# Start addresses of the weight blocks in the on-chip ring

## The reference

```
x = x + mixed(h @ w_in) @ w_out
x = x + memory_cross_attention(h, mem_n, w_xq, w_xkv, w_xo)
x = x + (silu(gate) * up) @ w_down        # gate, up = split(conv(h @ w_up) + bias)
x = x + (fox_attention(...)  * silu(gate)) @ fox_w_out
x = x + (swa_attention(...)  * silu(gate)) @ swa_w_out
```

## Time and profile before

| | |
|---|---|
| timed runs, us | 2169.78, 2170.08, 2170.18 (median 2170.08) |
| span of the profiled execution, us | 2167.6 |
| TensorE matmuls, busy | 2156.3 us, 13406 instructions |
| VectorE, ScalarE busy | 1618.3 us, 1327.2 us |
| read from HBM | 384.34 MB |

### The profile page before, as it was taken

How to read it: one execution, slowest core, us unless ns; L and a number is a source line. 1 busy time by engine, 2 the same in 40 slices (tenths; PEclk the granted TensorE clock), 3 DMA queues, 4 the chain that set the end, 5 groups by cost and what they waited for, 6 DMA issues and landing times.

```text
span 2167.6 us, 34503 instructions
## 1 busy us (share of the span) xinstructions
PE 2156.3 (99%) x13406; PEld 1865.8 (86%) x13406; DVE 1618.3 (75%) x2945; ACT 1327.2 (61%) x2601; POOL 9.7 (0%) x22
## 2 busy tenths in 40 slices
PE   9999999999999999999999999999999999999998
PEld 8888888888888888888888888888888888888887
DVE  7898666786688877655778867777676767688774
ACT  7866447775576666544666656555556655567764
POOL 0000000000000000000000000000000000000000
PEclk9999999999999999999999999999999999999999
DMA  7443434665455555555555555545554455544453
GB/s 279 169 146 137 147 115 141 218 217 186 156 190 189 188 191 186 193 185 192 187 191 189 185 194 185 193 171 197 181 177 174 167 192 186 189 161 155 146 200 140
DMA packets 107619, 389.31 MB, mean 180 GB/s; under 512 B 12304, under 2 KB 12560, under 8 KB 106688
## 3 DMA queue, kind: packets, MB, share of 16 engines
q1 hardware_dynamic: 105264, 377.31, 50.2%
q0 software_dynamic: 1904, 9.47, 1.2%
q10 hardware_dynamic: 288, 0.32, 0.0%
HBM read 384.34 MB, written 2.13 MB: 178 GB/s over the span
## 4 chain that ended last, share of the span: by engine, by line
PE 95%; DVE 3%; ACT 1%; issue 0%; DMA 0%; SPq 0%; DVEq 0%; ACTq 0%
PE main L510 88%; PE two L510 6%; PE two L513 1%; DVE WL L987 1%; DVE gt L987 0%; DMA RAW<-ws 0%; DVE GQ L993 0%; ACT L1654 0%; ACT WH L1655 0%; DVE GK L993 0%; PE main L556 0%; ACT PP L1655 0%; DVE PB L987 0%; ACT NT L1655 0%; DVE PP L993 0%
## 5 line engine op out<-in xcount | busy, mean ns | idle before, releaser
L1655 ACT ACTIVATE WH<-RAW 128x512 fp32r<-128x512 f32 x1416 | 882.1, 629 | 657.6 <-PE main L510 651.1
L987 DVE TENSOR_TENSOR WL<-RAW,WH 128x512 fp32r<-128x512 f32 x1416 | 961.2, 687 | 383.9 <-ACT WH L1655 374.4
L510 PE MATMUL main<-A,WH 128*128 128x512 f32 (+1 forms) x3680 | 1141.9, 393 | 1.0 <-DVE WL L987 1.0
L510 PEld LDWEIGHTS main<-A,WL 128*128 128x128 f32 x3584 | 673.9, 188 | 154.8
L510 PE MATMUL main<-A,WL 128*128 128x256 f32 x3584 | 713.7, 278 | 0.0
L510 PEld LDWEIGHTS main<-A,WH 128*128 128x128 f32 x3680 | 562.7, 189 | 13.8 <-issue 9.3
L510 PE MATMUL main<-H,WH 128*128 128x512 f32 x704 | 221.1, 395 | 0.0
L510 PE MATMUL main<-B,WH 128*128 128x512 f32 (+1 forms) x640 | 184.4, 373 | 0.0
L510 PEld LDWEIGHTS main<-H,WL 128*128 128x128 f32 x704 | 132.3, 188 | 31.3
L510 PE MATMUL main<-H,WL 128*128 128x256 f32 x704 | 138.4, 278 | 0.0
L510 PE MATMUL main<-WH,A 128*128 128x512 f32 (+1 forms) x448 | 137.6, 380 | 0.0
(11 more groups left out here) (322 smaller groups left out, 1722.5 us busy)
## 6 DMA issues: line engine op xcount, KB each, us to landing
RAW<-ws SPq DMA_DIRECT2D x707, 512.0 KB, 3.3
CB<-cscr POOLq DMA_DIRECT2D x4, 1024.0 KB, 4.7
XT<-xT POOLq DMA_DIRECT2D x4, 512.0 KB, 6.0
MS<-memT POOLq DMA_DIRECT2D x4, 512.0 KB, 8.7
xs<-xT SPq DMA_DIRECT2D x7, 256.0 KB, 7.6
out<-YT SPq DMA_DIRECT2D x7, 256.0 KB, 2.6
CST<-cst SPq DMA_DIRECT2D x1, 1248.0 KB, 7.9
G<-g POOLq DMA_DIRECT2D x1, 1024.0 KB, 5.9
```

Of the source, the lines that this page charges most:

```text
L510: return e.matmul(o, l, r, start=start, stop=True, skip_group_check=True)
L987: return e.tensor_tensor(o, a, b, op)
L1655: return e.activation(o, i, f, bias=bias, scale=scale, accum_out=accum)
```

## The change

The two rings become one tile W of six slots of 1088 values (4352 bytes, 17 x 256), each with room for the hi and the lo part. Tokens halves lie at 0 and 512 in a slot, which keeps the residue modulo 256 of before; plain and small halves at 16 and 528 (64 bytes further). In a wide half the four hi blocks lie in two runs of 256 values: the two of t = 1 from value 36, the two of t = 0 from 304; the lo blocks from 560 (t = 1) and 828 (t = 0). With a base at 128 modulo 256 the blocks start at 64 (hi, t = 0), 16 (hi, t = 1), 112 (lo, t = 0) and 64 (lo, t = 1). The host packs the wide weights in the order in which they are written, and ScalarE and VectorE write each half as two runs of 256 with a gap. To make room, RB, RB2, SM and RAW start 0.75 KB lower. The number of matmuls, their order and all waits stay.

```diff
--- before.py
+++ after.py
@@ -14,6 +14,9 @@
 T = 256
 EPS = 1e-6
 NRAW, NW, HI_AHEAD, LO_AHEAD = 5, 6, 5, 4
+PITCH = 1088
+ROW = {"tokens": (0, 512), "plain": (16, 528), "small": (16, 528)}
+PAIR = ((304, 36), (828, 560))
 MINI = {"ba": 16, "ff": 32}
 LNEXP = "natural_log_exp_and_others"
 SILU = "silu_and_others"
@@ -147,8 +150,13 @@
             v = w[r0:r0 + rows, c0:c0 + 512].reshape(k // 2, 2, 128, 512).transpose(0, 2, 1, 3)
             out[at:at + k // 2] = v.reshape(k // 2, 128, 1024)
         else:
-            v = w[r0:r0 + rows, c0:c0 + 512].reshape(k // 4, 4, 128, 2, 256).transpose(3, 0, 2, 1, 4)
-            out[at:at + k // 2] = v.reshape(k // 2, 128, 1024)
+            v = w[r0:r0 + rows, c0:c0 + 512].reshape(k // 4, 2, 2, 128, 2, 2, 128)
+            for part in range(2):
+                a = at + part * (k // 4)
+                x = v[:, :, :, :, part].transpose(0, 3, 1, 2, 4, 5)
+                if form_of(key, part) == "wide":
+                    x = x.transpose(0, 1, 2, 4, 3, 5)[:, :, :, ::-1]
+                out[a:a + k // 4] = x.reshape(k // 4, 128, 1024)
         at += k // 2
     assert at == total
     return out
@@ -319,10 +327,29 @@
         SQ, ACC, ACC2, SQ2 = at("SQ", 134, [4, T]), at("ACC", 138, [4, T]), at("ACC2", 142, [4, T]), at("SQ2", 128, [4, T])
         CST = at("CST", 146, [C_ROPE + 512])
         PAR = at("PAR", 156, [P_END])
-        RB, RB2 = at("RB", 160, [T]), at("RB2", 161, [T])
-        SM = at("SM", 162, [256])
-        RAW = at("RAW", 163, [NRAW, 1024])
-        WH, WL = at("WH", 163 + 4 * NRAW, [NW, 512], R), at("WL", 163 + 4 * NRAW + 2 * NW, [NW, 512], R)
+        RB, RB2 = at("RB", 159.25, [T]), at("RB2", 160.25, [T])
+        SM = at("SM", 161.25, [256])
+        RAW = at("RAW", 162.25, [NRAW, 1024])
+        W = at("W", 162.25 + 4 * NRAW, [NW * PITCH + 16], R)
+
+        def whole(j, lo):
+            o = PITCH * (j % NW) + ROW[form_of(*HALVES[j][0:2])][lo]
+            return W[:, o:o + 512]
+
+        def stationary(j, lo, r, t):
+            o = PITCH * (j % NW) + 128 * r + PAIR[lo][t]
+            return W[:, o:o + 128]
+
+        def written(j, lo):
+            if form_of(*HALVES[j][0:2]) != "wide":
+                return whole(j, lo)
+            o, gap = PITCH * (j % NW), PAIR[lo][0] - PAIR[lo][1]
+            o += PAIR[lo][1]
+            return W[:, o:o + 2 * gap].rearrange("p (t x) -> p t x", t=2)[:, :, 0:256]
+
+        def loaded(j):
+            x = raw(j)
+            return x.rearrange("p (t x) -> p t x", t=2) if form_of(*HALVES[j][0:2]) == "wide" else x
 
         M, MS = at("M", 80, [16, 2, T], R), at("MS", 112, [16, T])
         MH, ML = M[:, :, 0, :], M[:, :, 1, :]
@@ -543,7 +570,8 @@
                 w.wait_ge(s_lo, j + 1)
                 if i == 0 and c >= 2:
                     w.wait_ge(s_evac, c - 1)
-                P, h, l = slots[c % 2], WH[:, j % NW, :], WL[:, j % NW, :]
+                P = slots[c % 2]
+                h, l = (None, None) if form == "wide" else (whole(j, 0), whole(j, 1))
                 first = i == 0
                 if key[:2] == "w2" and first:
 
@@ -560,11 +588,10 @@
                     for r in range(2):
                         X = need(key, 2 * i + r)
                         both, hi = fl(X[:, 2 * i + r, :, :]), X[:, 2 * i + r, 0, :]
-                        cols = [slice(256 * r + 128 * t, 256 * r + 128 * t + 128) for t in range(2)]
                         for t in range(2):
-                            mm(P[:, t, :], h[:, cols[t]], both, start=first and r == 0)
+                            mm(P[:, t, :], stationary(j, 0, r, t), both, start=first and r == 0)
                         for t in range(2):
-                            ins = mm(P[:, t, 0:T], l[:, cols[t]], hi, start=False)
+                            ins = mm(P[:, t, 0:T], stationary(j, 1, r, t), hi, start=False)
                 elif key == "w23" and i >= n - NW:
 
                     for t in range(2):
@@ -573,7 +600,7 @@
                         for kt in range(n - NW, n) if t else (i,):
                             X = need(key, kt)
                             hi, lo = (X[:, kt, a, 128 * t:128 * t + 128] for a in range(2))
-                            kh, kl = (W[:, (j - i + kt) % NW, :] for W in (WH, WL))
+                            kh, kl = (whole(j - i + kt, a) for a in range(2))
                             mm(P[:, t, :], hi, kh, start=False)
                             mm(P[:, t, :], hi, kl, start=False)
                             ins = mm(P[:, t, :], lo, kh, start=False)
@@ -995,7 +1022,7 @@
             def lo(j):
                 if j < NH:
                     w.wait_ge(s_hi, j + 1)
-                    tt(WL[:, j % NW, :], raw(j), WH[:, j % NW, :].bitcast(F), ALU.subtract).then_inc(s_lo, 1)
+                    tt(written(j, 1), loaded(j), written(j, 0).bitcast(F), ALU.subtract).then_inc(s_lo, 1)
 
             def lo_of(L, H, kt, x, g):
                 return stt(L[:, kt, :], x, g, H[:, kt, :].bitcast(F), ALU.mult, ALU.subtract)
@@ -1665,7 +1692,7 @@
                         w.wait_ge(s_rawf, 16)
                     if j >= NW:
                         w.wait_ge(s_mm, j - NW + 1)
-                    copy(WH[:, j % NW, :], raw(j)).then_inc(s_hi, 1)
+                    copy(written(j, 0), loaded(j)).then_inc(s_hi, 1)
 
             def squares(stage, n, src):
```

## The result

The changed kernel takes 2173.49 us (median of 20 runs, 2171.23 to 2174.38) against 2169.98 us (20 runs, 2169.19 to 2170.58). The ratio is 1.0014, its interval 1.0008 to 1.0021: slower by 3.5 us. That is clear of the noise, and still within the 0.2% that was to count as no change. The forecast was 2121.7 us with a range to 2172, and the time lies 1.5 us above that range. The gain of 48 us is not there.

The account below looks back on a forecast made before the run. TensorE's matmul spacing was taken as the bound: 2167.6 us profiled, less 44.6 (wide) and 3.8 (plain), gives 2119.2; plus 2.5 carried over to the timed median, 2121.7 us. Range 2072 to 2172 us.

Parts of the forecast that it names:

- What bounds the kernel: Whole kernel: it ends when TensorE has issued its matmuls, busy 2156.3 of 2167.6 us; only their spacing is worth anything.
- Residues matter at all: TensorE's matmuls: cost above the columns depends on how moving operand and next weight block fall against each other.
- The rival of no effect: Matmul spacing: the residue isn't what spreads the times; 2170.1 us, between 2166 and 2174; chance 0.22.
- The wide term, 44.6 us: Wide form's 2384 steps: hi matmul at 227 ns, lo at 112, step 678 instead of 696.7 ns, saving 44.6 us.
- The bounds: Wide step: 646.6 ns with bare hi columns and lo at a 110 ns load; 712 with every matmul like the slowest.
- Worse conflicts: Wide form, lo matmuls above all: one of four new load-stream relations may be bad; 36.5 us lost, 2206.6 us; chance 0.13.
- Plain, 3.8 us: 480 plain and small matmuls of 256 columns: 112 instead of 120 ns each, 3.8 us saved.
- Tokens 0: Tokens form: its halves stay where they were, 0 gained; pieces must stay at 21.8 us for 96 matmuls.
- two runs 0: Tile written in two runs with a gap: 0 to 4 ns on VectorE, hidden; 5.7 us if that cover were gone.
- larger slots 0: Larger slots, moved RB, SM and RAW, new host order: same transfers, same waits, same six slots; 0.
- no new waits: TensorE's waits, 4.2 us before, should stay under 10 us.
- What is late next: VectorE: its share in 600 to 800 rises from 82% to 84%; in the first 400 us at most 9 us become waits.

Follow-up runs that it names:

- the layout run: Changed kernel with all blocks, wide and plain, back at the moving tile's residue, new layout and two-run writes kept: 2169.96 us, ratio 0.9998.
- the hi run: Changed kernel with only the wide form's hi blocks at the new residues, lo blocks at the moving tile's: 2189.4 us, ratio 1.0089.
- lo blocks alone: Changed kernel with only the wide form's lo blocks at the new residues, hi blocks at the moving tile's: 2175.06 us, ratio 1.0023.
- one pair of breaks: Changed kernel plus two extra small matmuls, 26 and 32 columns, four halves apart at the start of the feed-forward stretch: 2155.62 us, ratio 0.993.
- the last two: Changed kernel with one residue other, no extra matmuls: hi t = 1 at 96 bytes over the moving tile's, 2146.91 us; lo t = 0 at 0, 2175.39 us.
- (12, 6, 15, 12): Changed kernel with the hi block of t = 1 at 96 instead of 144 bytes over the moving tile's residue, no extra matmuls: 2146.91 us, ratio 0.9896.
- the scans: Two kernels with the feed-forward stretch in 63 groups of eight halves, each with other residues, two extra matmuls a group: between 2191 and 2201 us.
- (12, 9, 15, 12): The changed kernel: hi t = 0, hi t = 1, lo t = 0, lo t = 1 in 16-byte units over the moving tile's residue; 2173.49 us.

## Why the prediction was wrong

- **What bounds the kernel**: right. Only the spacing moved, and every kernel's time followed from it. For the change: of the undisturbed halves 93% cost 6.7 ns more and 6% 33.3 ns less; taken over to all 1192 wide halves that is +7.4 and -2.4 us. With 1.4 us gained in the plain and small forms it makes 3.6 us; measured are 3.5 in the medians and 4.4 in the spans.
- **Residues matter at all**: right, shown by the layout run (0.9998) beside the hi run (1.0089). The rival of no effect, 2166 to 2174 us, holds the measured time, but for a wrong reason: the near equality is a balance of a slow and a fast pattern. The Trainium skill has two independent read ports in TensorE ("SBUF — State Buffer", Who interferes with whom). That can't be the whole story here, since only addresses differ between these kernels and a half takes 1360 to 1414 ns. Where in the chip this happens, no run shows.
- **The wide term, 44.6 us: the step that failed.** I took 227 and 112 ns as the nearest rows below the mean, so 678 ns a step. The fast pattern is just that: 226.5 and 113.5, 680 ns a step. The size was right and the share of time wrong: I let one residue have one time. The trace had the 274, 278 and 283 ns of equal instructions; I read them as a collision that the residue would remove, but that is what a locked pattern looks like. That alone doesn't say how many patterns there are: the old residues have these durations too, and only one half time, breaks or not. No row of before could tell of two, and the sum took one time for all 2384 steps without a reason. The measured gain in that pattern is 33 ns a half x 60 halves, 2 us, not x 1192, and 913 halves lose 6.7 ns each instead.
- **The bounds**: 646.6 and 712 ns a step. The kernels with fixed residues went from 680 to 707 (1360 to 1414 a half), inside both. The lower one was loose: bare columns at 2.4 GHz were never reached.
- **Worse conflicts**, with a chance of 0.13 and priced at 36.5 us: the mechanism that won in the long piece (700 ns a step), at a fifth of its price. Its condition, that one of the four relations is bad, didn't describe it: one set of relations gives both patterns, and hi blocks alone are worse than all four together.
- **Plain, 3.8 us**: mis-sized, 1.4 us measured. Over all plain and small matmuls with no other one between, the mean distance fell from 119.9 to 116.9 ns, where 112 was assumed; for 480 that is 1.4 us. The first chunk's timeline (the first line below) now has 36 matmuls in 4.40 us, and one alone lasts 0.28, so they are (4.40 - 0.28) / 35 = 0.118 us apart. The piece of 272 matmuls that holds `xo` fell from 36.97 to 36.23 us; 0.42 of it is the plain form, 118.3 ns for 120.5, and the rest eight fast wide halves. The small form went to 113.6 ns. In four other kernels with the same plain residues (lo blocks alone, one pair of breaks, and the last two) `xo` runs at 114.0 ns, so the plain form has more than one pattern too.
- **Tokens 0, two runs 0, larger slots 0, no new waits**: right; 21.78 us for 96 (the chain's line below) as in the earlier trace rows; TensorE's waits 6.5 us in all, below the 10 allowed for.
- **What is late next** was never tested by the change itself. With (12, 6, 15, 12), 23 us faster, TensorE waits 7 us in all. In the run with one pair of breaks 437 halves in a row take 1360 ns, the pace that was forecast, and TensorE waits 6.3 us in all. So VectorE carries that pace there; the whole 48 us were never reached.

```profile
14.83 4.40 PE L537 MATMUL main<-A,W 128*128 128x256 f32 x36
```

```profile
2097.95 21.78 PE main L537 x96
```

- **Range and chances**: 0.22 for no effect was too little and the upper end of 2172 too tight. The prediction itself gave no effect up to 2174 us and said that the range kept it whole, and yet the range ended at 2172; the measured time lies in that gap. The loss rival was known and priced, too.

## What to carry to other kernels

Where one instruction stream repeats a fixed pattern for hundreds of microseconds, ask not only what a step costs but in how many patterns it can lock and what puts it there: equal instructions with two or three exact durations in a trace are a sign of a locked pattern, though not of a second one. A gain found in a short loop is the gain of one pattern; count in the real kernel's trace what share of the steps has it. And between a setting with the best time and one with a slightly worse time that nearly every interruption leaves as it is, the second won here, by 27 us.

## What the runs showed of the hardware

- The start residues of stationary blocks modulo 256 bytes, in steps of 16, change the spacing of matmuls with nothing else changed: 1360 to 1414 ns for a wide half in kernels with one setting, up to 1427 for single halves of the scans.
- The spacing is locked: 1400 ns for 526 halves in a row. It is switched by a small matmul of 26 and one of 32 columns (0.5 us, 18 us gained), and it was lost where one matmul took 16 ns longer.
- The same instructions can run in different patterns in different executions: 18 to 45 fast halves of the same 154.
- The lowest mean seen in any form is 1360 ns for 3072 columns, 226.7 for 512 (tokens: 21.78 us / 96 = 226.9) and 113.3 for 256. At the granted clock of 1.00, 2.4 GHz, that is 3264 cycles, 17 for every 16 columns. Single distances go down to 223 and 111 ns, with longer ones beside them. The Trainium skill ("TensorE: Matmul & The Clock Gate", Back-to-back issue gap) has columns over 2.4 GHz plus 2.5 ns for an isolated matmul, 215.8 and 109.2; no matmul with these fp32r operands came there. What the seventeenth cycle is, and whether it is one, stays open.
- Also open: what gives way in the slow patterns, the moving operand or the weight load, and whether (12, 9, 15, 12) can be made to restart in its fast pattern everywhere. With all 1192 wide halves there it would be some 40 us under the kernel before (33.3 ns each); it was not reached.
